# A change of order in the matmuls of a two-model kernel: each weight tile with 512 latent and 256 context columns in turn

## What is computed

```python
h = rms_norm(x, norm_g) * (1 + scale[:, None]) + shift[:, None]
hc = rms_norm(xc, norm_g) * (1 + scale_c) + shift_c
aq, ak, av, az, bq, bk, bv, bo, bz, bg, cq, ck, cv, cz, gm = split_proj(h @ w_in)
aqc, akc, avc, azc, bqc, bkc, bvc, boc, bzc, bgc, cqc, ckc, cvc, czc, gmc = split_proj(hc @ w_in)
...
x = x + gate[:, None] * merge_branches((y_a, y_b, y_c), gm, w_br, w_out)
if update_ctx:
    xc = xc + gate_c * merge_branches((y_ac, y_bc, y_cc), gmc, w_br, w_out)
```

## Time and profile before

| | |
|---|---|
| median of the 3 runs shown | 2966.46 us (2966.22 to 2968.91) |
| the profiled execution: its own time, from the first to the last instruction (span) | 2965.5 us |
| instructions | 38348 |
| PE busy | 2901.6 us, 98% |
| PE weight loads (overlap PE) | 2393.2 us, 81% |
| DVE busy | 1477.4 us, 50% |
| ACT busy | 1163.9 us, 39% |
| POOL busy | 146.0 us, 5% |
| granted TensorE clock, mean | 0.997 of full |

### The profile page before, as it was taken

How to read it: one execution, slowest core, us unless ns; L and a number is a source line. 1 busy time by engine, 2 the same in 40 slices (tenths; PEclk the granted TensorE clock), 3 DMA queues, 4 the chain that set the end, 5 groups by cost and what they waited for, 6 DMA issues and landing times.

```text
span 2965.5 us, 38348 instructions
## 1 busy us (share of the span) xinstructions
PE 2901.6 (98%) x15438; PEld 2393.2 (81%) x15438; DVE 1477.4 (50%) x2051; ACT 1163.9 (39%) x1856; POOL 146.0 (5%) x199
## 2 busy tenths in 40 slices
PE   9999999999999999999999999999999999999998
PEld 7778888776788887877888788868888788888776
DVE  5655455546463657366252543263455735453454
ACT  5444333526452344146233431173232743341452
POOL 1000000110000000100000300100001000200100
PEclk9999999999999999999999999999999999999999
DMA  5343332331332222210112221311113022321322
GB/s 185 122 158 105 113 128 85 129 130 38 136 107 98 99 87 76 82 54 22 60 43 76 85 68 57 101 60 64 57 64 101 21 82 78 108 91 66 121 75 85
DMA packets 48844, 260.98 MB, mean 88 GB/s; under 512 B 6872, under 2 KB 7904, under 8 KB 24896
## 3 DMA queue, kind: packets, MB, share of 16 engines
q1 hardware_dynamic: 36288, 213.75, 20.8%
q0 software_dynamic: 12416, 45.25, 4.5%
HBM read 250.50 MB, written 4.28 MB: 86 GB/s over the span
## 4 chain that ended last, share of the span: by engine, by line
PE 91%; DVE 4%; ACT 3%; DMA 1%; issue 1%; POOL 0%; SPq 0%; DVEq 0%; ACTq 0%
PE PS L897 15%; PE PS L898 15%; PE PS L899 15%; PE PS L874 7%; PE PS L876 7%; PE PS L875 7%; PE PS L833 3%; PE PS L835 3%; PE PS L834 3%; PE PS L1124 2%; PE PS L1086 1%; PE PS L1197 1%; PE PS L1179 1%; PE PS L1166 1%; PE PS L944 1%
## 5 line engine op out<-in xcount | busy, mean ns | idle before, releaser
L897 PE MATMUL PS<-HHX,WHX 128*128 128x512 f32 (+1 forms) x1440 | 504.6, 350 | 0.4 <-DVE WLX L2409 0.3
L898 PE MATMUL PS<-HL,WHX 128*128 128x512 f32 (+1 forms) x1440 | 503.4, 350 | 0.0
L1680 ACT ACTIVATE WHX<-W 128x2048 fp32r<-128x2048 f32 (+1 forms) x102 | 174.8, 1713 | 560.9 <-DMA W<-in_w 379.2
L899 PE MATMUL PS<-HHX,WLX 128*128 128x512 f32 (+1 forms) x1008 | 350.1, 347 | 0.0
L2409 DVE TENSOR_TENSOR WLX<-W,WHX 128x2048 fp32r<-128x2048 f32 x60 | 137.5, 2292 | 344.9 <-ACT WHX L1680 344.8
L897 PEld LDWEIGHTS PS<-HHX,WHX 128*128 128x128 f32 x1440 | 272.7, 189 | 38.3 <-DVE WLX L2409 1.5
L898 PEld LDWEIGHTS PS<-HL,WHX 128*128 128x128 f32 x1440 | 272.7, 189 | 34.9
L874 PE MATMUL PS<-HH,WH 128*128 128x512 f32 x672 | 261.7, 389 | 0.0
L876 PE MATMUL PS<-HH,WL 128*128 128x512 f32 x672 | 261.7, 389 | 0.0
L875 PE MATMUL PS<-HL,WH 128*128 128x512 f32 x672 | 261.6, 389 | 0.0
L2409 DVE TENSOR_TENSOR WL<-W,WH 128x2048 fp32r<-128x2048 f32 x68 | 155.7, 2290 | 177.8 <-ACT WH L1680 177.7
(11 more groups left out here) (553 smaller groups left out, 5813.8 us busy)
## 6 DMA issues: line engine op xcount, KB each, us to landing
W<-in_w SPq DMA_DIRECT2D x172, 1024.0 KB, 4.8
XC<-in_wm POOLq DMA_DIRECT2D x12, 1024.0 KB, 5.2
H<-in_wm POOLq DMA_DIRECT2D x12, 1024.0 KB, 6.0
W<-in_wb SPq DMA_DIRECT2D x24, 512.0 KB, 3.3
W<-in_w SPq DMA_DIRECT2D x8, 768.0 KB, 4.1
ARENA<-ARENA POOLq DMA_DIRECT2D x32, 128.0 KB, 2.3
ARENA<-mrow SPq DMA_DIRECT2D x12, 256.0 KB, 3.9
PR<-in_nbias POOLq DMA_DIRECT2D x12, 256.0 KB, 3.0
```

What stands on the lines that cost most here:

```text
L897: pe.matmul(dst, wh[:, s, c], hi[:, k, t0:t1], start=k == 0, stop=False)
L898: pe.matmul(dst, wh[:, s, c], lo[:, k, t0:t1], start=False, stop=False)
L899: mm = pe.matmul(dst, wl[:, s, c], hi[:, k, t0:t1], start=False, stop=k == kb - 1)
L1680: act.activation(dst[:, s, 0:n], W[:, s, 0:n], ACT.Copy).then_inc(wh_ready[s], 1)
```

## The change

Where a stage has context and both parts are asked for, `pe_split_unit_x` hands over to a new function. In it the part is the innermost loop: for each of the three products of a k-tile, the matmul over 512 latent columns is followed by the one over 256 context columns with the same weight tile, the first into bank 2s+m, the second into its half of bank 4+s. Both banks are open for the length of a half. PE waits for bank 4+s ahead of the slot's first matmul. `full[2s+m]` is signalled at the last latent matmul of the half, `slab_used[s]` at the last context matmul of the slot. The calls with one part at a time and the stages without context are as before. The per-tile waits on the low parts stand ahead of six matmuls where they stood ahead of three. The scores inside cz come after both parts of (s, m) = (1, 0).

```diff
--- before.py
+++ after.py
@@ -880,6 +880,9 @@
                         na=None, done=0):
 
         _, _, wh, wl, _ = split_bufs(st)
+        if st.ctx and len(parts) == 2:
+            pe_split_unit_both(pe, st, u, hi, lo, ready, kb, slots, ms, na)
+            return
         for s in slots:
             pe.wait_ge(wl_ready[s], u + (st["ws"] + 1))
             for t0, t1 in parts[:1 + st.ctx]:
@@ -905,6 +908,35 @@
                     if na and (s, t0, m) == (1, 0, 0):
                         wait_free(pe, na, 1, 0)
                         pe_na_scores(pe, na, na.steps[0])
+
+    def pe_split_unit_both(pe, st, u, hi, lo, ready, kb, slots, ms, na):
+
+        _, _, wh, wl, _ = split_bufs(st)
+        lat, both = slice(0, T), (slice(0, T), slice(T, TA))
+        for s in slots:
+            pe.wait_ge(wl_ready[s], u + (st["ws"] + 1))
+            for m in ms:
+                wait_free(pe, st, 2 * s + m, u)
+                if m == 0:
+                    wait_free(pe, st, 4 + s, u)
+                dsts = PS[:, 2 * s + m, :], PS[:, 4 + s, m * TC:(m + 1) * TC]
+                for k in range(kb):
+                    if s == slots[0] and m == 0:
+                        pe.wait_ge(ready[0], ready[1] + k)
+                    if st.after_norm and u == 0 and m == 0:
+                        pe.wait_ge(sem("ctx_lo"), KT * st.layer + k + 1)
+                    c = slice(k * SLAB + m * P, k * SLAB + m * P + P)
+                    for w, x_, first, last in ((wh, hi, k == 0, False), (wh, lo, False, False),
+                                               (wl, hi, False, k == kb - 1)):
+                        for dst, cols in zip(dsts, both):
+                            mm = pe.matmul(dst, w[:, s, c], x_[:, k, cols], start=first, stop=last)
+                            if last and cols == lat:
+                                mm.then_inc(full[2 * s + m], 1)
+                if m == 1:
+                    mm.then_inc(slab_used[s], 1)
+                if na and (s, m) == (1, 0):
+                    wait_free(pe, na, 1, 0)
+                    pe_na_scores(pe, na, na.steps[0])
 
     def pe_up(pe, st):
 
```

## The result

The changed kernel is **slower**: 2982.78 us, the median of 4 runs (2981.81 to 2985.22), against 2967.47 us for the kernel before (4 runs, 2966.22 to 2968.91; the 2966.46 of the prediction is the median of three of them). The ratio is 1.0054, 95% interval 1.0040 to 1.0068. Its profiled execution has a span of 2980.1 us, 14.6 more than the 2965.5 of before.

What follows compares the result with a forecast made beforehand. PE's matmul stream, number of matmuls times start-to-start distance, was taken as the bound; 0 - 0.8 + 0.7 + 0.7 = +0.6 us gave 2967 us, no measurable change, range 2949 to 2979.

Steps and rivals of the forecast that it cites:

- part 1: 2016 context matmuls move behind 512-column ones, loads stay 15438: pair term 0, block borders that go away -0.8 us.
- saving and extra cancel within each pair: Alternating pairs: what the 256 saves, the 512 behind it pays, so a pair stays 0.3467 us; term 0.
- the two borders: Block borders in the old trace: 256s behind a 512 0.005 to 0.01 us shorter, 512s behind a 256 0.005 longer.
- the second rival: All 2016 pairs: long matmuls never settle, +0.005 us each, +10 us, 2977 us; decides from 0.0026 per pair; chance 0.23.
- the waits of 1.4: PE's longer waits at the neighbourhood attention and at the row sums after mres, +0.7 us each.
- The first rival: In alternation the long matmul covers the short one's load for good: -15 us + 0.6, 2952 us; chance 0.19.
- the prediction's bound: Lower bound for the pairs: the 256's saving stays and nothing is paid back, -0.0075 x 2016 = -15 us.
- The third: Second matmul on a tile goes without a load; 0.013 us falls away 2016 times, -27 us, 2940 us; chance 0.03.
- Part 2: Slot ends: slab release, DMA and split chain don't move; ACT and DVE empty bank 2s+1 while awaiting the slab; cost 0.
- Part 3: Wait for context bank 4+s moves to the slot's start, covered in bo and merges; mres splits ready in time; cost 0.
- Part 4: Two tails grow: scores after cz wait for bank 3, row sums after mres for another DVE pass; +0.7 us each.
- pairs at 0.350 or more: Sign that the forecast is wrong: 512 and 256 pairs at 0.350 us or more, where it expected 0.347.

Runs made afterwards that it cites:

- the half order: Changed kernel, but each half of a slot runs its 24 matmuls of 512 columns, then its 24 of 256; 2966.59 us, ratio to before 1.0003.

## Why the prediction was wrong

**The step that failed** is in part 1: "saving and extra cancel within each pair", which made the term 0. A pair keeps the steady sum of 0.3467 us in the fast pattern alone, the 512s 0.2316 and the 256s 0.1151 on the average: there the extra and the saving do cancel, as I read the two borders. In the slow pattern the 512s take 0.2365 (0.0096 more than in the earlier trace rows) and the 256s 0.1168 (0.0030 less than in the earlier trace rows), so 0.0066 us of each pair stays, and 72 of 84 runs are of that kind. 10.5 us in place of 0 less 0.8.

What happened is the second rival, the long matmuls that never settle. Its sign and its place were right: +0.005 a pair and 10 us were forecast, 0.0066 and 10.5 measured, well past its point of 0.0026. That the sizes meet is in part luck: the rival had the 512s at +0.005 with nothing saved at the 256s, and every pair alike; measured are +0.0096 and -0.0030, in 72 runs of 84. I gave it 0.23, because the block borders can be read in two ways and I took the reading with one constant, which fitted both borders and both steady distances. Five long matmuls behind a border were evidence on how a new order begins, not on what it settles into; the question "into which steady state?" was not in those rows at all.

**The range** ended at 2979 us, a little past that rival's 2977, and was left by 3.8 us: the rival's 10 less 0.8 at the borders became 10.5, the waits of 1.4 became 1.55 (with the 0.44 at L833, which was not forecast), and 2.5 came from low-clock stretches at other places and small waits, for which the range had no term.

**The first rival** is refuted. (Its point is 6.5 / 2016 = 0.0032, not 0.0033; nothing hangs on it.) The Trainium skill ("TensorE: Matmul & The Clock Gate", section "Architectural detail: the array is 16× 32×32, not 1× 128×128") lets the queue pull weight loads ahead of matmuls in flight. By that rule a pair would have become shorter, by the 0.0075 us of the prediction's bound; in strict alternation with full loads none was under 0.3467. The trace agrees no further than before: in the changed kernel, too, a load starts with the matmul ahead of its own, and no earlier. Here the weight loads of the first stretch shown above (a row of x2 is the load for a long matmul and the one for a short):

```profile
1206.82 0.31 PEld L932 LDWEIGHTS PS<-HL,WHX 128*128 128x128 f32 x2
1207.18 0.31 PEld L932 LDWEIGHTS PS<-HHX,WLX 128*128 128x128 f32 x2
```

The load at 1206.82 belongs to the long matmul of 1206.93 and begins with the short one ahead of it. The third, a load that falls away, is refuted by the 15438 loads.

**Part 2** holds as far as it was seen: DVE has 3.7 and ACT 0.7 us less to do than before, and no wait for a bank appeared. One slab came 0.44 us late at L833, where its low part was in time before; that wait shows in the half order too (0.88 us) where 24 matmuls of one length stand together, so the alternation is not needed for it; what moved it was not followed.

**Part 3**, cost 0, is right. PE's waits in the changed kernel list L932 only for the low part of two merges' first slab, as L897 before, and the half order kept the early wait for bank 4+s at a ratio of 1.0003:

```profile
PE PS L932 <- DVE WLM L2441: 0.7, 2, 0.4
```

**Part 4** is right in place and nearly in size: 0.7 us forecast at each tail, 0.57 measured at the neighbourhood attention and 1.25 - 0.71 = 0.54 at the row sums.

Of the signs that I named, the loads (15438), the missing wait at slot starts and the two tails came as forecast, and "pairs at 0.350 or more" was the sign of the error that came. Slots didn't keep their 16.6 us: in the slow pattern a slot of two runs takes 16.96.

## What to carry to other kernels

A stream of matmuls without any wait can still change its time with the order alone: here 512 and 256 columns in strict alternation took 0.3533 us a pair in most blocks, and the same columns in blocks of one length, or as 384 and 384, 0.347. Sharing a weight tile between two matmuls saved no load, so there was nothing to set against that price; keep matmuls of one length together, or cut them equal. When a trace has no place where two shapes alternate, its borders bound the price but don't tell the steady state: a range should then reach past the worse border.

## What was not expected of the hardware

- One and the same instruction stream has two steady paces, 0.3467 and 0.3533 us a pair (8.32 and 8.48 us a run of 48), with no wait and at the same granted clock; an execution takes one on entering a block of strict alternation and, where nothing breaks the order, keeps it for up to 864 matmuls. That alone moved the unedited kernel's span by 2.9 us between two executions.
- 512 with 384 columns paid more than 512 with 256 (0.0133 against 0.0067 us a pair in most blocks), though the lengths are closer; 384 with 384 paid nothing.
- 64 in place of 128 weight columns for the long matmuls took a pair to 0.3400 us, below the 0.3467 of the fast pattern; for the short ones all pairs took 0.3467. Neither kernel had two patterns.
